# VectorE's extra steps behind its copy of the turned rows, in both attention loops of a three-block transformer kernel

## The reference

```python
s = jnp.einsum('bgmqd,bgnd->bgmqn', qb, kc)
p_cmp = masked_softmax(s, cmp_end[None, :] <= tq[:, None])
o_cmp = jnp.einsum('bgmqn,bgnd->bgmqd', p_cmp.astype(vc.dtype), vc)
...
o = jnp.stack([o_cmp, o_sel, o_win], axis=-1).reshape(b, NSA_HEADS, Q_BLOCK, d, 3)
return jnp.einsum('bhqdc,bhqc->bqhd', o, gb)
```

```python
s = s + ci[..., None] - c_k[:, :, None, :]
s = jnp.where(k_pos[None, :] <= q_pos[:, None], s, NEG_INF_2)
p = jax.nn.softmax(s, axis=-1)
return jnp.einsum('bhqk,bkhd->bqhd', p.astype(v.dtype), v)
```

## Time and profile before

| What | Value |
|---|---|
| Median of 3 runs | 1878.94 us (1878.88 to 1879.91) |
| The profiled execution | 1878.52 us |
| Its span, first to last instruction | 1876.4 us |
| Instructions | 21689 |
| Mean granted clock of PE | 0.974 |
| First attention loop | 724 to 818 us of the span |
| Second attention loop | 1390 to 1478 us of the span |
| Busy in the span: PE, DVE, ACT, POOL | 94%, 40%, 30%, 12% |

### The profile page before, as it was taken

The page is one execution under the profiler, slowest core; times in us unless marked ns, Lnnn a source line. Parts: engine busy times, 40 slices in busy tenths (PEclk is TensorE's granted clock), DMA queues, the critical chain, the costliest instruction groups (busy, mean ns, idle before and its releaser), DMA issues. The chain is left out here.

```text
span 1876.4 us, 21689 instructions
## 1 busy us (share of the span) xinstructions
PE 1768.7 (94%) x9017; PEld 1303.1 (69%) x9017; DVE 753.2 (40%) x1113; ACT 558.5 (30%) x857; POOL 232.2 (12%) x278
## 2 busy tenths in 40 slices
PE   7998999999999999998999999999999978999993
PEld 6777888888878786567888888878776663333331
DVE  5445223233365345736222233253347463333334
ACT  5235222232352124636222232262247310000001
POOL 3000000000002003310000000000014303333322
PEclk9999999999999998999999999999999977999997
DMA  7222433322232217212333322333320166999984
GB/s 235 91 68 69 111 89 89 109 93 90 90 118 90 83 55 235 80 46 62 96 89 101 101 90 91 111 113 90 90 90 24 53 249 267 355 398 395 377 322 148
DMA packets 179409, 260.46 MB, mean 139 GB/s; under 512 B 18872, under 2 KB 134776, under 8 KB 167040
## 3 DMA queue, kind: packets, MB, share of 16 engines
q1 hardware_dynamic: 155824, 204.66, 32.5%
q0 software_dynamic: 19472, 25.29, 4.4%
q10 hardware_dynamic: 4032, 29.36, 4.0%
HBM read 297.05 MB, written 29.40 MB: 174 GB/s over the span
## 5 line engine op out<-in xcount | busy, mean ns | idle before, releaser
L149 DVE TENSOR_TENSOR RING_R<-RING,RING_R 128x2048 fp32r<-128x2048 f32 (+1 forms) x110 | 250.3, 2277 | 619.9 <-ACT RING_R L146 619.8
L168 PE MATMUL PB<-RING_R,OPS_R 128*128 128x512 f32 (+1 forms) x1056 | 414.6, 393 | 10.1 <-DVE RING_R L149 5.8
L170 PE MATMUL PB<-RING_R,OPS_R 128*128 128x512 f32 (+1 forms) x1056 | 409.1, 387 | 0.0
L169 PE MATMUL PB<-RING_R,OPS_R 128*128 128x512 f32 (+1 forms) x1056 | 409.0, 387 | 0.0
L146 ACT ACTIVATE RING_R<-RING 128x2048 fp32r<-128x2048 f32 (+1 forms) x110 | 208.4, 1897 | 299.8 <-DMA RING<-in_ffn_w_down 137.3
L168 PE MATMUL PB<-OPS_R,RING_R 128*128 128x512 f32 (+1 forms) x736 | 281.8, 383 | 7.8 <-DVE OPS_R L275 7.8
L169 PE MATMUL PB<-OPS_R,RING_R 128*128 128x512 f32 (+1 forms) x736 | 281.3, 382 | 0.0
L170 PE MATMUL PB<-OPS_R,RING_R 128*128 128x512 f32 (+1 forms) x736 | 281.2, 382 | 0.0
L168 PEld LDWEIGHTS PB<-RING_R,OPS_R 128*128 128x128 f32 x1056 | 199.0, 188 | 53.8 <-DVE RING_R L149 8.5
L170 PEld LDWEIGHTS PB<-RING_R,OPS_R 128*128 128x128 f32 x1056 | 198.8, 188 | 40.9
L169 PEld LDWEIGHTS PB<-RING_R,OPS_R 128*128 128x128 f32 x1056 | 199.0, 188 | 38.9 <-issue 0.2
(11 more groups left out here) (353 smaller groups left out, 1877.0 us busy)
## 6 DMA issues: line engine op xcount, KB each, us to landing
RING<-in_ffn_w_gate SPq DMA_DIRECT2D x44, 512.0 KB, 4.0
RING<-in_ffn_w_up SPq DMA_DIRECT2D x44, 512.0 KB, 5.2
RING<-in_ffn_w_down SPq DMA_DIRECT2D x44, 512.0 KB, 4.1
RING<-in_w_expert_gate SPq DMA_DIRECT2D x16, 1024.0 KB
RING<-in_w_expert_up SPq DMA_DIRECT2D x16, 1024.0 KB
OPS<-in_w_expert_gate SPq DMA_DIRECT2D x16, 1024.0 KB
OPS<-in_w_expert_up SPq DMA_DIRECT2D x16, 1024.0 KB
Y<-in_w_expert_down ACTq DMA_DIRECT2D x14, 1024.0 KB
```

What stands on the lines that cost most here:

```text
L149: nc.vector.tensor_tensor(RING_R[:, raw], RING[:, raw], RING_R[:, high].bitcast(fp32), ALU.subtract).then_inc(s_wlo, 1)
L168: nc.tensor.matmul(o, x[0], w[0], start=start, stop=False)
L169: nc.tensor.matmul(o, x[0], w[1], start=False, stop=False)
L170: return nc.tensor.matmul(o, x[1], w[0], start=False, stop=stop)
```

## The change

In step u of both loops DVE's copy of head 1's turned rows is issued before the extra steps and no longer after them. In the first loop the steps in `RET_AT` and `SPLIT_AT` are numbered one higher, which moves the turning of the retention rows on PE, and ACT's high parts and its half of the split, one step later too; DVE's part of them, at `u - 1`, is then behind the copy of one unit later. `OUT_AT` stays.

```diff
-        RET_AT = {11: 4, 13: 5, 19: 6, 21: 7}
+        RET_AT = {12: 4, 14: 5, 20: 6, 22: 7}
...
-        SPLIT_AT = {14: 1, 22: 2}
+        SPLIT_AT = {15: 1, 23: 2}
...
                 normed(u)
                 if u + 2 < NU:
                     maxima(u + 2)
+                dve.wait_ge(*a_t.at(2 * u + 2))
+                w = width(u)
+                nc.vector.tensor_copy(PTn[u % 2][:, 1, 0:w], PB[:, 5, 0:w]).then_inc(a_pb.sem, 1)
                 if u == 2:
...
                 if u - 1 in SPLIT_AT:
                     split_to(dve, "dve", d_od.n0 + SPLIT_AT[u - 1])
-                dve.wait_ge(*a_t.at(2 * u + 2))
-                w = width(u)
-                nc.vector.tensor_copy(PTn[u % 2][:, 1, 0:w], PB[:, 5, 0:w]).then_inc(a_pb.sem, 1)
...
+                dve.wait_ge(*t_tr.at(2 * u + 2))
+                w = width2(u)
+                nc.vector.tensor_copy(PT2[u % 2][1][:, 0:w // P, :].rearrange("p k n -> p (k n)"), PB[:, 5, 0:w]).then_inc(t_pb.sem, 1)
                 if u >= 6 and u % 4 == 2:
                     y2_low(dve, u // 4 - 1)
                 if u == SUMS_AT + 2:
                     split_to(dve, "dve", d_2.n0 + 3)
-                dve.wait_ge(*t_tr.at(2 * u + 2))
-                w = width2(u)
-                nc.vector.tensor_copy(PT2[u % 2][1][:, 0:w // P, :].rearrange("p k n -> p (k n)"), PB[:, 5, 0:w]).then_inc(t_pb.sem, 1)
```

## The result

| | before | after |
|---|---|---|
| Median, run beside each other, 6 runs each | 1879.34 us (1878.66 to 1881.47) | 1887.92 us (1886.4 to 1891.6) |
| Ratio, 95% interval | | 1.005 (1.004 to 1.006) |
| The profiled execution | 1878.52 us | 1890.35 us |
| Its span | 1876.4 us | 1888.2 us |
| Mean granted clock of PE | 0.974 | 0.972 |

The changed kernel is slower by 8.6 us, 0.5%, where 7.6 were forecast; its median lies 1.4 us above the predicted 1886.5 and inside the range.

What follows compares the result with a forecast made beforehand. PE, busy 94% of the span, was taken as the bound; 1.1 + 2.4 + 0 + 3.7 + 0.4 = 7.6 us on the profiled 1878.52 gave 1886.1, plus 0.4 for the median 1886.5 us; range 1881.5 to 1891.5.

Steps and rivals of the forecast that it cites:

- The mechanism: Both loops: a step behind the copy delays the next unit's reciprocals and scalings, so PE's transposes wait; 7.6 us in all.
- Weight splits, 1.2 each: First loop, splits now behind copies of units 16 and 24: transposes of 17 and 25 later, 2.4 us for two.
- The rest of the first loop, 0: First loop, low parts and retention rows' turning moved: priced at 0, between -0.5 and +1.0 for each of two rounds.
- The split's length: Moved weight split, both loops: takes the short 2.29 us, GpSimd being idle; with 2.45 each place costs 0.17 more.
- The compressed sum, 1.1: First loop, unit 2: sum ends 1.08 us later, PE waits 1.6 instead of 0.5 before unit 3's transposes; 1.1 us lost.
- The low parts of the second loop, 3.7: Second loop, units 6 to 30: six times 0.57 us and 0.25 for unit 26; 3.7 us lost, range 2.5 to 4.3.
- The split of the second loop, 0.4: Unit 24: the 1.00 us wait at the values goes, about 1.7 comes at unit 25's transposes; 0.4 us lost.
- The clock: Forecast: clock as now. Rival, chance 0.28: one to three falls at new waits add 1.4 to 4.2 us, 1887.9 to 1890.7.
- theory 1: The prediction's own account, both loops: moved steps delay the next unit's reciprocals and scaled rows; terms add up to 7.6 us.
- Nothing outside the loops: Nothing outside 724 to 1478 us of the span changes in length.

Runs made afterwards that it cites:

- a_split1: Kernel before with only the first loop's two weight splits one step later, VectorE's half behind the copy, ScalarE's half included: 1882.77 us, ratio 1.0022.
- a_low1: Kernel before with only the first loop's low parts behind the copy and the retention rows' turning one step later: 1881.07 us, ratio 1.0008.
- a_low2: Kernel before with only the second loop's low parts moved behind the copy: 1880.88 us, ratio 1.0011.
- a_split2: Kernel before with only the second loop's weight split moved behind the copy of unit 24: 1878.68 us, ratio 1.0003.
- a_sum: Kernel before with only the compressed sum moved behind the copy of unit 2: 1880.85 us, ratio 1.0011.
- b_fill_before: Kernel before with 7 unread identity transposes on PE ahead of the values of unit 24, second loop: 1876.68 us, ratio 0.9984.
- b_fill: Changed kernel with 8 to 12 unread identity transposes on PE in each of four new waits: 1883.56 us, ratio 1.0021 to before.
- d_low_gap: Changed kernel with the second loop's low parts one unit later, ahead of the copy of units 7, 11, ...: 1885.01 us, ratio 1.0037 to before.

## Why the prediction was right, point by point

**The mechanism.** Right at the places that it named, but for the compressed sum, whose price was read from a stretch at half clock. In after, PE's wait at the values of 14 is down from 0.76 to 0.23 and at 15 it is gone, and the transposes of 17 wait. PE, DVE and POOL of after, the rows that answer to the earlier trace rows:

```profile
771.80 1.09 PE L1483 MATMUL PB<-Z 128*64 128x128 f32 x16 [0.23 <-DVE Z L1604]
774.80 1.09 PE L1483 MATMUL PB<-Z 128*64 128x128 f32 x16
779.89 0.91 PE L1460 MATMUL PB<-ident,Z 128*128 128x128 f32 x2 [0.98 <-POOL Z L1631]
...
776.93 2.28 DVE L149 TENSOR_TENSOR RING_R<-RING,RING_R 128x2048 fp32r<-128x2048 f32 x1
779.13 0.16 DVE L1584 RECIPROCAL nsa_scale<-nsa_den 128x2 f32<-128x2 f32 x1
779.39 0.88 POOL L1631 TENSOR_SCALAR Z<-Z,nsa_scale,gate_s 128x128 f32<-128x128 f32 x2 [3.09 <-DVE nsa_scale L1584]
```

Read from the split down: 776.93 + 2.20 = 779.13, reciprocals, GpSimd 0.26 later, its first half 0.44, PE 0.06 behind that at 779.89. That is the forecast's chain, link by link, and its wait of 0.98 was forecast as about 1.1.

**Weight splits, 1.2 each.** Units 5 to 31 cost 2.79 at full clock, 1.33 in the first round. The books inside this were kept loosely. I kept 0.1 of the 0.46 at the values of 15 because the transposes of 16 would wait; PE is 0.48 earlier there, counted from the turning, and gave 0.11 to the transposes' start and 0.32 to their length, which leaves 0.05. From the transposes of 16 to those of 17 the moved split costs 1.06 in a_split1 (3.65 against 2.59) where I had 1.05 (3.64), and 0.32 more for head 1's rows.

**The rest of the first loop, 0.** Right in the sum, for the reason given: the 0.5 of the turning took the place of the 0.76 at the values of 14 (they start 28.19 us after the turning of the compressed part, before 28.24). It is right only together with the split. The turning and the low parts cost 1.2 a round alone and 1.0 on top of the splits, at or beyond the upper end of the range given for them. So 2.4 for the splits and 0 for the rest is a right account of the time along the way, and not the worth of each part.

**The split's length.** 2.28 in after, with GpSimd idle from the step before. The long row, 2.45 in the earlier trace rows, had a scaling beside it for its first 0.31 us. The Trainium skill, "GPSIMD Engine Reference", Specifications, says that GpSimd and VectorE share their SBUF interfaces and contend when VectorE's instruction has two SBUF inputs, as the split has. The traces agree: the whole split takes 2.44 to 2.45 wherever such a scaling overlaps it (before, a_low1, a_low2, a_split2, a_sum, b_fill_before) and 2.28 to 2.29 wherever none does.

**The compressed sum, 1.1.** The term that was mis-sized most: 0.34 to 0.42. The step that failed is "the chain ends at 734.90 instead of 733.82". PE, DVE and POOL of after, answering to the earlier trace rows:

```profile
734.94 1.23 PE L1460 MATMUL PB<-ident,Z 128*128 128x128 f32 x4 [2.27 <-POOL Z L1631]
...
731.05 0.42 DVE L1604 COPY Z<-PB 128x256 f32<-128x256 f32 x1
731.39 1.21 DVE L1607 TENSOR_REDUCE cmp_den<-WK 128x32 f32<-128x1024 f32 x1
...
733.30 1.05 POOL L1643 TENSOR_TENSOR WK<-WK,cmp_den 128x512 f32<-128x512 f32 x1 [2.78 <-DVE cmp_den L1612]
```

In the earlier trace rows PE turns unit 2 at the half clock and ends at 732.78, 0.70 after the sum could start (732.08), so the copy, put first, would have had to wait for it, and the sum with it. In after the clock is up, the copy follows the maxima at once (731.05), and the sum is later by the copy's 0.34 alone. The 1.1 would hold only for an execution in which the clock rises as late as in the earlier trace rows, and no run shows one with the sum moved. "The copy's values were not waiting" is also true only there: in a_low1 they wait 1.20. That wait is won, but nothing comes of it, since the start of unit 3's transposes hangs on the sum. So the wait there is even longer than forecast (2.27 against 1.6), of which 1.20 stood at the copy before.

**The low parts of the second loop, 3.7.** Measured 3.11 alone. The gap and the six repeats were right, the last of them (unit 30) only where the clock holds. Inside a repeat errors cancelled. The low part takes 0.66 between its neighbours in the new place where I had 0.72. The slack was 0.23 and not 0.14, since from VectorE's scaling to PE it takes 0.06 (1419.12 + 0.55 = 1419.67, PE at 1419.73) and not the 0.15 read at a copy; so PE starts only 0.42 later. But head 1's rows are not quite in time, and the transposes take 0.13 longer. Unit 26 gave nothing in after, behind the low clock, and a seventh wait in b_fill at the full one. A group of four units takes 9.96 (values at 1418.50 and 1428.46) against 9.42: 0.54 against the forecast 0.57.

**The split of the second loop, 0.4.** Measured 0.32, with a wait of 1.67 (1.7 forecast) at the transposes of unit 25.

**The clock.** The forecast left it as it was and gave 0.28 to falls at the new waits. By after's trace this was too low a chance: of its five falls inside the loops three stand behind waits that I had named, units 17 and 25 of the first loop and 25 of the second. The one at 735 came also in a_low1 and a_split1, where the sum isn't moved. The one at 1483 stands behind waits of 0.91 and 0.74 for copies, which before has as well, without a fall:

```profile
1482.78 1.53 PE L1879 MATMUL PB<-Z 128*64 128x128 f32 x12 [0.74 <-DVE Z L1983]
```

At 779.89 the transposes of unit 17 follow a wait of 0.98, and the stretch behind them has:

```profile
780.00:781.00 1.00, 1.00 (x4) 0.53 (x6) 0.18 (x2) 0.39 (x2) 0.26 (x1) 0.50 0.00 0
```

The clock pays 1.5 to 1.7 us in the median, the low end of the rival's 1.4 to 4.2 and known to some 2 us; the terms of theory 1 came out 0.4 to 0.7 lower than forecast, and the two errors partly cancel. That 1886.5 lies so near 1887.9 is owed in part to that.

**Nothing outside the loops.** Right: 574.8 between them against 574.6.

## What to carry to other kernels

When a step is to be moved on an engine that isn't the bound, ask what it stands ahead of in the new place. In a software pipeline two handovers to the bound engine follow each other closely, and the step then pays at the second what it saves at the first. What wins is a gap in which the engine waits anyway, with the step cut to fit it: a split moved whole cost 0.3 to 0.4 us beside what the clock took, and the three in four pieces each gave back 2.2 us in the loops at full clock and 3.4 in the median. The price of a moved step depends on what moves with it, so parts timed alone need not add up. And a slack read from a stretch at a low clock isn't the slack that other executions have.

## What the runs showed of the hardware

**Short waits cost twice.** The granted clock of PE fell from full to half (2.4 to 1.2 GHz) after waits of about 1 us in otherwise dense work: 0.98 at 779.89 of after, 0.98 at 799.85 of a_split1, 1.00 and 0.20 in the earlier trace rows. It came back 3 to 7 us later. One fall cost 1.45 us in before (83.38 - 81.93) and 2.25 in a_split1 (2.66 - 0.41); the two falls in the second half of after's first loop cost 2.9 together (units 5 to 31 take 81.67, in b_fill 78.81).

**It doesn't fall at each such wait.** a_split1 has one wait of 0.99 and one of 0.98 with equal work around them; after the first the scores take 0.92, after the second 1.65. a_low1 has waits of 1.42 at full clock with no fall behind them. b_fill_before waits 1.26 at the values of unit 2 and 0.59 at the transposes of unit 3 without a fall; a_low1 waits 1.20 and 0.59 there and the clock falls. The fall at 735 us came in after, a_sum, a_split1 and a_low1, where the clock had first risen at 728, with the sum at its new and at its old place; it didn't come in the kernels where the clock rose at 730 or later, but for d_low_gap (risen at 733, fallen at 736). What decides wasn't found, and no run here was made for it.

**Dummy work holds the clock up.** 7 transposes of the identity ahead of one wait made the kernel before faster by 2.5 us (0.16%, interval 0.07% to 0.25%), although PE then does more.
